# A two-layer hybrid attention kernel: attention steps in another order, and the second layer's rows, roots and first weights made ready in the first layer's last products

## What is computed

```python
# N = 1088 rows: tiles 0..7 are 1024 prompt rows, tile 8 ("SAMPLE") 64 rows; D_MODEL = 1024, 2 layers
def layer(x, p, conv_buf, h0, past, lam_init):
    xn = rmsnorm(x, p['norm_pre'])
    proj = jnp.einsum('bld,de->ble', xn, p['w_in'])
    ...
    a_h, h_last = rg_lru(a_c, h0, ...)                 # branch A
    y_b = sweep_query_blocks(dsa_block ...)            # branch B: top-256 keys, 4 heads
    y_c = sweep_query_blocks(diff_block ...)           # branch C: two softmax maps a head, 4 heads
    ...
    mix = jnp.einsum('ble,ed->bld', jnp.concatenate([y_a, y_b, y_c], axis=-1), p['w_out'])
    x = x + rmsnorm(mix, p['norm_post'])
    return x, (new_buf, h_last, bk, bv, b_ik, ck, cv)
```

## Time and profile before

| | |
|---|---|
| Median of 3 timed runs | 1717.11 us (1715.88 to 1722.72) |
| The profiled execution's own time | 1713.17 us |
| Its span, first to last instruction | 1711.4 us |
| PE busy | 1579.6 us, 92% |
| DVE busy | 1130.6 us, 66% |
| ACT, POOL busy | 626.8 us, 425.3 us |
| Mean granted clock of TensorE | 0.973 |

### The profile page before, as it was taken

One profiled execution on the slowest core, in us unless ns is written; L12 is line 12 of the kernel. 1 busy time (PEld: TensorE's weight loads), 2 busy tenths in 40 slices (PEclk: granted clock), 3 DMA queues, 4 the chain that ended last, 5 costly groups with the idle time before them and its releaser, 6 DMA issues. The chain is left out here.

```text
span 1711.4 us, 21022 instructions
## 1 busy us (share of the span) xinstructions
PE 1579.6 (92%) x7276; PEld 1083.2 (63%) x7298; DVE 1130.6 (66%) x2456; ACT 626.8 (37%) x1227; POOL 425.3 (25%) x540
## 2 busy tenths in 40 slices
PE   6999999999988889999859999999999888899996
PEld 3566566688876755567435665666888667555663
DVE  3478999948963655465134789999589646545550
ACT  2285520228143333333022756202280433333330
POOL 2001621520020344342120016205200213444411
PEclk9999999999998999999979999999999999999999
DMA  5100001321050311110151000013210503111101
GB/s 175 53 25 25 25 25 50 100 76 35 1 185 4 113 38 58 40 38 32 49 187 53 25 25 25 25 50 99 65 47 0 183 6 117 42 52 37 51 24 56
DMA packets 39177, 99.19 MB, mean 58 GB/s; under 512 B 8672, under 2 KB 27616, under 8 KB 34720
## 3 DMA queue, kind: packets, MB, share of 16 engines
q1 hardware_dynamic: 39072, 97.85, 17.3%
HBM read 66.84 MB, written 18.14 MB: 50 GB/s over the span
## 5 line engine op out<-in xcount | busy, mean ns | idle before, releaser
L1551 PE MATMUL ps<-r_xn,r_w 128*128 128x384 f32 (+1 forms) x1728 | 555.3, 473 | 12.3 <-DVE r_xn L1218 7.5
L1551 PEld LDWEIGHTS ps<-r_xn,r_w 128*128 128x128 f32 x1728 | 326.0, 191 | 195.7 <-issue 18.5
L1319 DVE TENSOR_SCALAR_CACHE_REDUCE r_ix<-r_sc,smi 128x768 bf16<-128x768 f32 (+6 forms) x380 | 342.0, 962 | 2.2
L1141 ACT ACTIVATE r_sc<-ps,sm 128x1024 f32<-128x1024 f32 (+8 forms) x204 | 155.7, 764 | 346.4 <-DVE sm L1454 339.2
L1454 DVE TENSOR_REDUCE sm<-ps 128x1 f32<-128x1024 f32 (+8 forms) x204 | 157.2, 784 | 121.8 <-PE ps L1699 52.1
L1627 PE MATMUL ps<-r_w,r_xn 128*128 128x256 f32 x1024 | 223.4, 380 | 0.0
L1627 PEld LDWEIGHTS ps<-r_w,r_xn 128*128 128x128 f32 x1024 | 193.9, 190 | 27.3 <-issue 1.0
L1736 PEld LDWEIGHTS ps<-r_vg,r_w 128*128 128x128 f32 (+1 forms) x1176 | 149.9, 194 | 52.9 <-issue 25.4
L1736 PE MATMUL ps<-r_vg,r_w 128*128 128x64 f32 (+1 forms) x1176 | 151.9, 274 | 6.3 <-DVE r_w L613 3.0
L1717 PE MATMUL ps<-ident,r_sc 128*128 128x128 f32 (+1 forms) x684 | 118.0, 282 | 39.1 <-ACT r_w L570 28.1
L1775 PE MATMUL ps<-r_xn,r_ag 128*128 128x512 f32 x256 | 137.5, 644 | 14.4 <-DVE r_res L1481 11.4
(11 more groups left out here) (244 smaller groups left out, 2068.5 us busy)
## 6 DMA issues: line engine op xcount, KB each, us to landing
r_w<-w_in SPq DMA_DIRECT2D x28, 1024.0 KB, 4.9
r_xn<-w_out SPq DMA_DIRECT2D x2, 4096.0 KB, 13.5
y<-r_res SPq DMA_DIRECT2D x16, 512.0 KB, 2.9
r_vg<-x SPq DMA_DIRECT2D x8, 512.0 KB, 9.9
r_xn<-ckT SPq DMA_DIRECT2D x2, 2048.0 KB, 8.3
r_xn<-vcache SPq DMA_DIRECT2D x2, 2048.0 KB, 13.8
o_v<-r_vg SPq DMA_DIRECT2D x4, 1024.0 KB, 11.1
r_sc<-x SPq DMA_DIRECT2D x8, 512.0 KB, 4.9
```

What stands on the lines that cost most here:

```text
L1141: ins = nc.scalar.activation(ex[2 * (i % 2) + m][0:r, 0:w], on_slot(s, w, r), ACT.Exp, bias=negm[0:r, c:c + 1], accum_out=den[0:r, c:c + 1])
L1319: ins = vec.tensor_scalar(unsel[t][0:rows(t), :], sc[t][0:rows(t), :], b, None, op, ALU.add, accum_out=cnt[0:rows(t), c:c + 1])
L1551: ins = nc.tensor.matmul(on_ring(key, cn), w[:, k, P * s:P * (s + 1)], xnT[:, k, c0:c0 + cn], start=(k == 0), stop=(k == KT - 1))
```

## The change

**Order of the attention steps.** `exp`, `comb` and `div` become steps of their own. `divide` of a unit stands directly behind its `pv`; for tiles of up to 512 keys it so comes ahead of the second map's maximum (C) or of the emptying of `tbank` (B). For the sample tile the scores of the unit after next stand between the first and second transpose group. `ytr` stands ahead of the unit's transposes instead of behind them. The product of n = 7 starts only after the last unit (16 steps at the end where there were 14).

**Three places for the product.** `mixb` becomes `mixbs`: banks 4 and 5 for n = 1 and 3, banks 0 and 1 for n = 7, banks 2 and 3 for the others. A product waits for the last one that had the same place. `rows` follow one or two units later than before. To make room, odd score slots of tiles up to 512 keys move to bank 1.

**The layer's boundary.** SP issues, behind the last `pv` of the first layer, the loads of x tiles 0, 1, 2, of the second layer's first weight unit, of `cst`, and of x tiles 3, 6, 7, 8. ACT squares these tiles, POOL makes their roots and DVE scales them during the last two products. Tile 4 (n = 7) is squared and scaled straight from `res`. The `square` and `rows` of tile 5 (n = 8) move behind the barrier into the second layer, which begins with PE's transposes.

```diff
 def take(i, most):
     new = []
     while waiting and most and i >= hold[0]:
-            n, q = waiting.pop(0)
+            n, q = waiting[0]
+            if n >= NT - 2 and i < len(units):
+                break
+            waiting.pop(0)
...
             if q == proj_steps(ORDER[n]) - 1:
                 new.append(("square", n))
-                finish.append(n)
-                hold[0] = i + 2
+                late = 1 if width(units[min(i, len(units) - 1)][0]) > BANK else 2
+                finish.append((i + late, n))
+                if mix_place(n + 1) == mix_place(n):
+                    hold[0] = i + late + 1
...
+    deferred = [("square", NT - 1), ("rows", NT - 1)] if has_next else []
...
+                    if has_prev:
+                        load_unit(1)
+                        r0 = P * LATE
+                        sp.wait_ge(carry_res, 1)
+                        sp.dma_start(y[r0:r0 + P, :], res[:, :]).then_inc(carry_stored, 16)
...
+                        elif s == ("pv", len(ATT) - 1) and has_next:
+                            sp.wait_ge(o_filled, len(ATT))
+                            sp.wait_ge(y_stored, 16 * (NT - 2))
+                            for t in EARLY_X[0]:
+                                load_next(t)
+                            sp.dma_start(ring[0], w_in[layer + 1, 0]).then_inc(w_next, 16)
+                            sp.dma_start(cst[:, :], acst[layer + 1]).then_inc(cst_next, 16)
+                            for t in EARLY_X[1]:
+                                load_next(t)
...
+                    if has_next:
+                        sp.wait_ge(w_next, 16)
+                        sp.wait_ge(cst_next, 16)
+                        sp.wait_ge(xres_in, 16 * NT)
+                    sp.wait_ge(y_stored, 16 * (NT - len(deferred) // 2))
...
# POOL, second layer's start
+                    if has_prev:
+                        b = (NT - 1) % 2
+                        pool.wait_ge(carry_sso, 1)
...
+                        pool.wait_ge(carry_mix, 1)
+                        nc.gpsimd.tensor_tensor(res[:, :], res[:, :], xres[:, :], ALU.add).then_inc(carry_res, 1)
+                        root_x(LATE, 1)
+                        pool.wait_ge(carry_stored, 16)
+                        pool.wait_ge(xs_ready, 1)
+                        nc.gpsimd.memset(r_res[:, :], 0.0).then_inc(wg_zero, 1)
...
# ACT, behind the ytr of n = 8 in the first layer
+                            if has_next and n == NT - 1:
+                                for k, tt in enumerate(EARLY_X[1]):
+                                    act.wait_ge(x_in[tt], 16 if has_prev else 32)
+                                    square_x(tt, base + len(EARLY_X[0]) + k + 1, xt[tt])
+                                act.wait_ge(res_ready, NT - 1)
+                                square_x(NEXT_LATE, base + NT - 1, res)
...
# DVE, second layer's front, in the loop over t
+                        if has_prev and t == 3:
+                            dve.wait_ge(carry_rso, 1)
+                            vec.scalar_tensor_tensor(res2[:, :, :], mixbs[mix_place(NT - 1)], rso[:, b:b + 1],
+                                                     gpost2[:, :, :], ALU.mult, ALU.mult).then_inc(carry_mix, 1)
+                        if has_prev and t == 4:
+                            scale_x(LATE, 1, res)
...
# PE
                             if part == 0:
-                                if n:
-                                    pe.wait_ge(mix_drained, n)
...
+                                if same_place(n):
+                                    pe.wait_ge(mix_drained, same_place(n)[-1] + 1)
```

More of the change, by code:

```diff
@@ L91 @@
 YTR = 2
+NARROW_MIX = (1, 3)
+LATE, NEXT_LATE = ORDER[-1], ORDER[-2]
+EARLY_X = [[0, 1, 2], [t for t in range(3, NT) if t not in ORDER[-2:]]]
+NARROW_END = 7
 LAST_ROWS = [("tm", "cv", 3), ("tm", "cv", 4)]
@@ L129, in schedule, with scores @@
     hold = [FIRST[ORDER.index(SAMPLE) + 1] + FIRST_PROJ]
-    def qk(i):
-        return [("qk", i, m) for m in range(maps_of(i))]
+    begun = [0]
+    def scores(i):
+        new = []
+        if begun[0] <= i < len(units):
+            begun[0] = i + 1
+            if i:
+                new.append(("comb", i - 1))
+            for m in range(maps_of(i)):
+                new += [("qk", i, m), ("exp", i, m)]
+        return new
     def take(i, most):
@@ L150, in schedule @@
         groups = [("tr", i, g) for g in range(-(-nk // 4))]
[L151 to L152 removed]
+        rows_now = [("rows", finish.pop(0)[1])] if finish and finish[0][0] <= i else []
         quota = QUOTA.get(t, 0)
[L154 to L162 removed]
+        pv = [("pv", i - 1), ("div", i - 1)] if i else []
+        n = NTH[i]
+        ytr = []
+        if i - FIRST[n] == YTR and n:
+            ytr = [("ytr", n - 1)]
+        nxt = scores(i + 1)
+        if not nxt:
+            nxt = [("comb", i)]
+        if len(groups) == 1:
+            steps += nxt[:3] + take(i, 1) + pv + rows_now + nxt[3:] + ytr + take(i, quota - 1) + groups
+        elif t == SAMPLE or (False and kind == "B"):
+            steps += nxt
+            steps += rows_now + ytr + take(i, 1) + groups[:1]
+            ahead = []
+            if i + 2 < len(units) and maps_of(i + 1) == maps_of(i + 2) == 1:
+                ahead = [("qk", i + 2, 0), ("exp", i + 2, 0)]
+                begun[0] = i + 3
+            steps += ahead[:1] + take(i, quota - 1) + (groups[1:2] + pv if ahead else pv + groups[1:2])
+            steps += groups[2:] + ahead[1:]
+        else:
+            steps += rows_now + nxt + ytr + take(i, 1) + groups[:1] + take(i, quota - 1) + pv + groups[1:]
+        if ytr:
             waiting += [(n - 1, q) for q in range(proj_steps(ORDER[n - 1]))]
@@ L165, in schedule @@
     hold[0] = last
-    steps.append(("pv", last - 1))
-    steps += [("rows", n) for n in finish]
+    steps += [("pv", last - 1), ("div", last - 1)]
+    steps += [("rows", n) for _, n in finish]
     while waiting:
@@ L170, in schedule @@
         new = take(last, 2 * KT)
-        steps += new + ([("rows", new[-1][1])] if new[-1][0] == "square" else [])
-    steps.append(("ytr", NT - 1))
+        steps += new + ([("rows", new[-1][1])] if new[-1][0] == "square" and new[-1][1] < NT - 2 else [])
+    steps += [("ytr", NT - 1), ("rows", NT - 2)]
     waiting += [(NT - 1, q) for q in range(proj_steps(ORDER[-1]))]
@@ L749, in _ @@
                             sp.dma_start(wo, w_out[layer]).then_inc(wo_in, 16)
-                        elif s[0] == "rows":
+                        elif s[0] == "rows" and s not in deferred:
                             store(s[1])
```

165 lines of the change are left out of this document (116 added, 49 removed).

## The result

The changed kernel takes 1724.6 us in the median (1718.8 to 1727.9, 20 runs) against 1716.2 us before (1707.0 to 1724.5, 20 runs). The ratio is 1.0054, 95% interval 1.0036 to 1.0071: slower by half a per cent, where 1672 was forecast, with 0.03 for slower.

What follows compares the result with a forecast made beforehand. PE, 92% busy, was taken as the bound. Gains of 21.0 + 3.5 + 1.5 + 19.0 = 45.0 us took the profiled 1713.2 to 1668.2, plus 3.9 for the timed median: 1672, range 1658 to 1691.

Steps and rivals of the forecast that it cites:

- What bounds the kernel: Whole kernel: PE, busy 92%, bounds it; time can come from its idle time, in attention and between layers, and its clock.
- A: Boundary between the layers: squares, roots, scalings and loads hidden under the last two products, 21.0 us gained (14 to 23).
- B: Start of the last product, both layers: DVE-read wait goes, 3.5 us gained, plus 1.5 from the clock.
- the half rate: First layer's last product: 8 records took 6.58 us against 3.70 in the second; half of the 2.9 us taken as gained.
- C, the attention: Attention steps of both layers: shorter PE waits, 9.5 us gained a layer, 19.0 in all (6 to 28).
- Narrow and wide tiles: Attention behind the sample tile: PE's idle 16.3 us a layer falls to 8.0, a gain of 8.3.
- six at 0.9 are 5.4: Six branch-C attention units left without product steps (40, 41, 48, 49, 56, 57) cost 0.9 us each, 5.4 a layer.
- the sample tile's 3.0 a layer: Sample tile's attention: four units in the new order keep one short wait each, 3.0 us gained a layer.
- Rival 1: Attention: denser product steps leave branch-C units bare and DVE bounds them; gain only 32 us, 1685; chance 0.19.
- Rival 2: Layer boundary: half its gain lost to late x tiles or unchanged first waits; 34 us gained, 1683; chance 0.10.
- rival 3: First layer's attention: the clock rises too, half of 16 us gained on top, 1664; chance 0.10.
- Rival 4: Attention: many short waits hold PE at half rate; granted 0.84 loses 76 us, near 1748; decides below 0.885; chance 0.04.

Runs made afterwards that it cites:

- e_dense: Old order of attention steps with the new layer boundary, plus the second and third bank places so product steps go in early: 1701.4 us, ratio 0.9910.
- e_narrow: Old order of attention steps with the new layer boundary, plus the new order inside the narrow tiles' units alone: 1683.1 us, ratio 0.9795.

## Why the prediction was wrong

**What bounds the kernel**: right in part. PE was idle where it said, but the 6.0 idle of 116 us at the end of the attention had little to give: the best kernel here has 3.9 in its late stretch where the kernel before has 4.3.

**A and B, the boundary and the last product**: right, in the sum and in the main steps. 21.0 + 3.5 + 1.5 = 26.0 were forecast, 26 measured with the attention unchanged, 24.5 with the new order (1.0197 less 1.0054). PE idled 0.82 us for 0.9 (of which the last quarter, "PE's pipeline", came of no row), and the first projection product came 5.6 us behind the product's end for 5.8. The wait of 1.3 us for `ytr` came as said, and the 8 records behind it took 3.67 us in the first layer, 6.58 before: the half rate went whole, where I took half. Why is not shown: of the two waits of 3.07 us before, one was followed by the lower level and one was not.

**C, the attention**: wrong in sign, -19 forecast and +35 measured. Two steps failed.

The first is the line "Narrow and wide tiles", where the gain was taken from waits that the new places remove, and nothing was charged for what the moved instructions pass on to the other engines. The copy of y was moved ahead on PE, and with it behind two exponentials on ACT (12.7 us). The rows were moved ahead of the combine on DVE (14.9 us), with the wait for their root and POOL's add beside the combine. Moving both back gave 27 of the 35.

The second is the term "six at 0.9 are 5.4". By the order of steps there are seven bare C units behind tile 6, 39, 40, 47, 48, 55, 56 and 65, and one before (unit 30); the prediction's numbers are one too high, and it left out unit 65. And the five in tiles 3 to 5 cost 2.7 us each, not the 0.9 of tile 6's. Of PE's idle time alone there is 9.1 us more in e_dense's late stretch, 1.8 a unit, and the clock falls from 1.00 to 0.97; part of it can be the rows that fall in these units. The gain in the narrow tiles pays for some of this, so the places alone cost 10.5 us net.

The two steps are bound together: the bank places cost 10.5 us in the old order, the new order without them 7, and both 35. The runs tell the larger part of these 17 us more: the places bring the rows out of B units into C units, where the new order puts them ahead of a combine, and that costs 14.9. PE's waits for the copy of y are as long with steps beside them.

The narrow tiles gave 9 us in e_narrow, of 16.6 forecast for narrow and wide; the sample tile's 3.0 a layer did not come: waits for DVE's reciprocals and the product behind one took the place of the waits removed. (The terms of that sum, 4 x 0.95 less 0.7, are 3.1.)

**The rivals.** Rival 1 named the mechanism, bare C units with DVE late, but bounded its cost at 2 us a unit, and its argument against, that DVE was busy for only 51 to 58%, is an average that says nothing of which instruction is behind which. Rival 2 did not come, the boundary's gain is whole; nor did rival 3: the clock over the first layer's attention (479.5 to 857.2 us) fell to 0.91, from 0.95 before. Rival 4, slower by the clock, came true in the sign and in part in kind: granted 0.84 in the late stretch, as it had supposed for the whole attention, but 0.91 over the first layer's. That is above its threshold of 0.885: it was costed alone against the whole gain, and idle time, which was said to fall, rose by 13.4 us in the late stretch.

**The range** reached to 1691 and so left out all cases in which C is a loss: its lower bound for C was +6. It should have been bounded below nothing, as the moved instructions' price on ACT and DVE was in no term.

## What to carry to other kernels

When steps are moved in a written order, write down for each engine what the moved instruction now stands behind, what now stands behind it, and what it waits for itself, since that wait is passed on; a place that is free on TensorE may be behind two exponentials on ScalarE. When a bank lets filler work start earlier, look at two things: which units it leaves without filler, and in which units the work behind the finished product (here the rows) now falls. Dealt anew, the same banks came with the fastest kernel here. And put an add on GpSimd where no two-input VectorE instruction that others wait for can fall on it.

## What the runs showed of the hardware

A combine on DVE (two inputs and output in SBUF) started 0.39 us after a 2.34 us add on POOL took 2.62 us instead of 0.88, and again 2.76 instead of 1.02; with the add held back they took 0.89 and 1.02. A small DVE instruction of this kind (L672, 128x64) took 0.71 us from 773.79 in the changed kernel, while a row of POOL instructions with two inputs in SBUF (L956) ran to 774.41, and 0.23 at 766.81 with POOL idle. Two maxima that read PSUM beside that add (from 755.16 us in the kernel with the add held back) took 1.55 us together, and 1.54 in the changed kernel (763.12) with POOL idle. The granted clock does not go by idle time alone: over the late stretch it was 1.00 with 4.3 us idle, 0.97 with 13.4 (the old order with early steps), 0.95 with 8.1 (the new order with steps where they were) and 0.84 with 17.7 (the change). What in the pattern of waits makes the difference was not tried.
